# The front of a fused two-block kernel: c alone on ScalarE's queue, an early table load, parameters turned behind x, the third weight tile one piece earlier, and sums of scale and shift by transposes

## The chip, the cores and the metric

The kernel runs on one core of a Trainium2 chip. The metric is the device time of one execution in microseconds, of which the median over several runs is taken. Before the change it is 1377.33 us (three runs, 1375.95 to 1377.88).

## What is computed

Two model blocks on one sequence of 512 tokens with 1024 channels, all float32. Only the first steps matter here:

```python
c_act = jax.nn.silu(c)                                # c: 1 x 1024
mod = (c_act @ w_mod[l] + b_mod[l])[:, None, :]       # w_mod: 1024 x 6144
sh1, sc1, g1, sh2, sc2, g2 = jnp.split(mod, 6, axis=-1)
h = rms_norm(x) * (1.0 + sc1) + sh1                   # x: 512 x 1024
proj = h @ w_in[l]                                    # 1024 x 10272
```

Behind them come a gated branch, a state space scan, three projections, a feed-forward part, and a second block with pooling and a recurrent branch. `sh1` and `sc1` take 8 MB of `w_mod`, and no matmul of `proj` can begin before at least one 128-channel piece of both is known.

## The kernel before

The program is written by hand, engine by engine: each engine has one function (`sp_program`, `pool_program`, `pe_program`, `act_program`, `dve_program`) that lists its instructions in order, and every engine works strictly through its own list. Semaphores tie the lists together. `s_...` names are semaphores; a wait is `wait_ge`.

**Layout.** Channels lie on the 128 partitions, in eight channel groups `m` of 128; tokens lie along the free axis. `XT` is x turned into that form. `h` is kept as two float32r tensors, `Hh` (high part) and `Hl` (the rest), and each weight tile of 1024x128 is split in the same way: `raw[i]` is what the DMA brings, ScalarE rounds it to `whi[i]` (`hi(t)`), VectorE subtracts to `wlo[i]` (`lo(t)`). A product is three matmuls per channel group: whi by Hh, whi by Hl, wlo by Hh. Three such tiles are in flight; the first three of the program (dt, cv 0, cv 1) are tiles 0, 1 and 2.

**The front** is everything up to the last matmul of these three tiles.
- SyncE (SP) issues nearly all loads: x in four pieces (`xnat`), then the pieces of `w_mod` (`wm`) in the order of `MOD_ROWS`, with tiles 0, 1 and 2 put in after pieces 1, 3 and 5 (counted from 0). Pieces 0 to 3 are 512 KB (128 columns each: scale and shift of channel groups 0 and 1), pieces 4 to 9 are 1 MB (256 columns, two channel groups each). Piece 4 is `wm5` (scale) and piece 5 is `wm1` (shift), both for channel groups 2 and 3. ScalarE's own DMA queue brings `c` and, once `c` is there, six small parameter vectors into rows of `pr[1]`.
- TensorE turns c (L808), then x in four calls `x_turned(c)` (L801), and the parameters (L814). `mod_rows(n)` multiplies piece n by silu(c) (L825); it leaves four partial rows in four groups of 32 partitions of a PSUM bank. ScalarE copies that bank to `mrow` (`mod_row(n)`, L1490), and `mod_sums(n)` (L834) multiplies `mrow` by a column `selc` that picks one partition of each group, which both adds the four partials and turns the row into a column. VectorE adds the biases (`h_cols(i)`, L2152 and L2154), scales XT (`h_scaled(m)`, L2166), ScalarE adds the shift and rounds (`h_hi(m)`, L1495), VectorE makes the rest (`h_lo(m)`, L2172).
- `part(t, k...)` (L853 to L855) is tile t's product for the channel groups k, three matmuls each: it waits for `whi`, `wlo`, and for `h_hi(k)` and `h_lo(k)`.
- `keep_busy` (L779) and `keep_busy_half` (L790) are 128x512 bf16 matmuls whose results nobody reads. Their number is written out in TensorE's list.
- The rms of x: ScalarE squares x (L1470), takes the root (L1483), VectorE inverts it (L2145), TensorE spreads it over the partitions (L842).

After the front the general loop `gemm` follows (L742 to L744), with the same three matmuls per channel group.

Of the kernel before, what the change touches and what calls it, by code (L numbers as in the profile page):

```python
# [7 lines left out]
F32R = mybir.dt.float32r  # L8
BF16 = mybir.dt.bfloat16
U8 = mybir.dt.uint8  # L10
ALU = mybir.AluOpType
# [25 lines left out]
def build_program(nc, A, out, blocks):  # L37
# [21 lines left out]
    selc = sb("selc", [P, 2])  # L59
# [55 lines left out]
    filler, = region(106, ("filler", [P, 512], F32R))  # L115
# [329 lines left out]
    def sp_program(sp):  # L445
# [30 lines left out]
        for p, piece in enumerate(MOD_ROWS):  # L476
            load_mod0(*piece)
            if p in (1, 3, 5):
                load((1, 3, 5).index(p))
# [91 lines left out]
    def pool_program(pool):  # L571
# [9 lines left out]
        for i in range(2):  # L581
            pool.tensor_tensor(selc[:, i:i + 1], ident[:, 64 * i:64 * i + 1], ident[:, 64 * i + 32:64 * i + 33],
                               ALU.add).then_inc(s_const, 1)
        pool.wait_ge(s_const, 7)
        pool.tensor_tensor(selc[:, 0:1], selc[:, 0:1], selc[:, 1:2], ALU.add).then_inc(s_const, 1)
        pool.tensor_copy(triub[:, :], triu[:, :]).then_inc(s_const, 1)
        for i in range(4):
            pool.tensor_copy(filler[:, i * 128:(i + 1) * 128], ident[:, :]).then_inc(s_const, 1)
# [127 lines left out]
    def pe_program(pe):  # L716
# [66 lines left out]
        def keep_busy_rounded(n, width, bank=5):  # L783
            for i in range(n):
                pe.matmul(BK[bank][:, 0:width], filler[:, i % 2 * 128:i % 2 * 128 + 128], filler[:, 0:width],
                          start=True, stop=True)

        def keep_busy_half(n, bank=5):
# [4 lines left out]
        def x_turned(c):  # L793
            pe.wait_ge(s_x[c], 16)
            half, at = divmod(c, 2)
            for b in range(4):
                if c == 2 and b == 3:
                    pe.wait_ge(s_pc, 3)
# [7 lines left out]
        keep_busy(4, 0)  # L806
        pe.wait_ge(s_par, 16)
        pe.transpose(BK[5][:, 0:8], pr[1][0:8, :], ident[0:8, 0:8]).then_inc(s_pt, 1)  # L808
        keep_busy(6, 0)
        x_turned(0)  # L810
        x_turned(1)
        pe.wait_ge(s_par, 16 * 7)
        pe.wait_ge(s_cact, 1)
        pe.transpose(BK[5][:, 128:256], pr[1][:, :], ident[:, :]).then_inc(s_pt, 1)  # L814
        x_turned(2)
        x_turned(3)

        def mod_rows(n):
            i, at, width = MOD_ROWS[n]
            if n >= 2:  # L820
                pe.wait_ge(s_mrow, n - 1)
            pe.wait_ge(*((s_wmr[i // 4], 32) if at else (s_wm[i], 16)))
# [6 lines left out]
        def mod_sums(n):  # L829
# [3 lines left out]
            for to, at in [(2 * (n % 2) + n // 2, 0)] if n < 4 else [(2 * n - 4, 0), (2 * n - 3, 128)]:  # L833
                ms = pe.matmul(BK[6][:, to:to + 1], mrow[n % 2][:, at:at + 128], selc[:, 0:1], start=True, stop=True)  # L834
            ms.then_inc(s_ms, 1)

        pe.wait_ge(s_const, 13)
        pe.wait_ge(s_xt0, 4)
        mod_rows(0)
# [19 lines left out]
        mod_rows(1)  # L859
# [2146 lines left out]
```

## Time and profile before

| | |
|---|---|
| median of 3 runs | 1377.33 us |
| the profiled execution's own time | 1375.54 us |
| its span, first to last instruction | 1374.3 us |
| TensorE busy | 1355.8 us, 99% |
| VectorE, ScalarE, GpSimd busy | 65%, 46%, 17% |
| front (last matmul of L855 starts) | at 49.06 us |

The span is 1.24 us shorter than the profiled execution's own time. That execution lies 1.8 us under the median of the three runs. Times in the rows below are microseconds from the start of the span. In the chain of waits a row is a stretch in which that engine, line or transfer is what everything behind it hangs on.

### The profile page before, as it was taken

What the parts mean: (1) busy time and instruction counts of PE and PEld (TensorE: products, weight loads), DVE (VectorE), ACT (ScalarE), POOL (GpSimd) and SP (SyncE); (2) the same over time, 40 slices, a digit from 0 to 9 for tenths busy, and PEclk for the clock granted to TensorE, in tenths of its full rate; (3) what the DMA queues carried; (4) which work ended last, traced back from release to release, by engine and by line L of the source; (5) the groups of instructions that cost most, each with busy time, mean ns of one, the idle gap of its engine ahead of it and who ended that gap; (6) DMA issues with size and microseconds to landing.
All of it is one profiled execution on the core that took longest, in us unless ns stands there. A gap on an engine that the chain in (4) does not pass through costs nothing.

```text
span 1374.3 us, 24508 instructions
## 1 busy us (share of the span) xinstructions
PE 1355.8 (99%) x9502; PEld 1095.3 (80%) x9502; DVE 896.9 (65%) x1274; ACT 628.8 (46%) x1000; POOL 239.9 (17%) x254
## 2 busy tenths in 40 slices
PE   8999999999999999999999999999999999999998
PEld 5788888888887888878888888888888877777776
DVE  4687777887637867784668542334444686867865
ACT  4565555665454523332245432123433465545533
POOL 0000000000037889860022500000000000000220
PEclk9999999999999999999999999999999999999999
DMA  9445344444445676553333333333333232313221
GB/s 346 135 140 140 115 116 130 138 108 128 141 138 157 165 205 195 153 166 95 93 92 93 108 92 108 92 93 94 106 93 92 73 112 60 88 51 92 64 73 77
DMA packets 276009, 163.46 MB, mean 119 GB/s; under 512 B 6573, under 2 KB 264242, under 8 KB 275898
## 3 DMA queue, kind: packets, MB, share of 16 engines
q1 hardware_dynamic: 269530, 158.90, 39.7%
q10 hardware_dynamic: 6368, 3.00, 0.8%
q8 instruction: 79, 1.29, 0.4%
q14 instruction: 32, 0.26, 0.1%
HBM read 159.59 MB, written 2.29 MB: 118 GB/s over the span
## 4 chain that ended last, share of the span: by engine, by line
PE 86%; DVE 6%; ACT 3%; issue 2%; POOL 2%; DMA 1%; ACTq 0%; DVEq 0%; SPq 0%; POOLq 0%
PE PS L742 23%; PE PS L744 22%; PE PS L743 22%; PE PS L942 1%; PE PS L1019 1%; POOL mbuf L607 1%; PE PS L1020 1%; PE PS L1021 1%; PE PS L1354 1%; PE PS L1356 1%; PE PS L1355 1%; PE PS L1257 1%; PE PS L1268 1%; POOL mbuf L602 1%; PE PS L963 1%
## 5 line engine op out<-in xcount | busy, mean ns | idle before, releaser
L742 PE MATMUL PS<-Hh,whi 128*128 128x512 f32 x1096 | 442.8, 404 | 2.6 <-DVE wlo L2113 2.3
L744 PE MATMUL PS<-Hh,wlo 128*128 128x512 f32 x1096 | 427.7, 390 | 0.0
L743 PE MATMUL PS<-Hl,whi 128*128 128x512 f32 x1096 | 427.2, 390 | 0.0
L2113 DVE TENSOR_TENSOR wlo<-raw,whi 128x1024 fp32r<-128x1024 f32 (+2 forms) x211 | 271.8, 1289 | 117.5 <-ACT whi L1457 116.6
L1457 ACT ACTIVATE whi<-raw 128x1024 fp32r<-128x1024 f32 (+2 forms) x215 | 222.6, 1036 | 171.9 <-PE PS L744 121.4
L742 PEld LDWEIGHTS PS<-Hh,whi 128*128 128x128 f32 x1096 | 205.8, 188 | 54.4 <-issue 10.8
L744 PEld LDWEIGHTS PS<-Hh,wlo 128*128 128x128 f32 x1096 | 205.7, 188 | 44.1
L743 PEld LDWEIGHTS PS<-Hl,whi 128*128 128x128 f32 x1096 | 206.1, 188 | 39.6 <-issue 0.7
L602 POOL TENSOR_TENSOR mbuf<-mbuf,cact 128x1024 f32<-128x1024 f32 x32 | 67.4, 2107 | 413.0 <-DMA mbuf<-in_w_mod_dram 407.0
L607 POOL TENSOR_TENSOR mbuf<-mbuf 128x512 f32<-128x512 f32 x68 | 99.7, 1466 | 5.3
L742 PE MATMUL PS<-YBh,whi 128*128 128x512 f32 x256 | 99.6, 389 | 0.0
L743 PE MATMUL PS<-YBl,whi 128*128 128x512 f32 x256 | 99.6, 389 | 0.0
L744 PE MATMUL PS<-YBh,wlo 128*128 128x512 f32 x256 | 99.6, 389 | 0.0
L702 POOL TENSOR_TENSOR pad<-pad 128x512 f32<-128x512 f32 x10 | 11.0, 1097 | 501.7 <-DVE VT L2617 501.2
L2260 DVE SCALAR_TENSOR_TENSOR tmp<-xr,pcA,tmp 128x512 f32<-128x512 f32 x96 | 71.8, 748 | 2.6 <-ACT tmp L1561 0.3
L1591 ACT ACTIVATE dec<-crow,dts 128x128 f32<-128x128 f32 x128 | 44.0, 393 | 31.5 <-PE PS L947 15.0
L742 PEld LDWEIGHTS PS<-YBh,whi 128*128 128x128 f32 x256 | 48.1, 188 | 10.0
L743 PEld LDWEIGHTS PS<-YBl,whi 128*128 128x128 f32 x256 | 48.1, 188 | 9.9
L744 PEld LDWEIGHTS PS<-YBh,wlo 128*128 128x128 f32 x256 | 48.1, 188 | 9.9
L2561 DVE TENSOR_TENSOR tmp<-tmp 128x512 f32<-128x512 f32 x30 | 20.9, 697 | 50.4 <-ACT tmp L1774 50.4
L742 PE MATMUL PS<-R2h,whi 128*128 128x512 f32 x128 | 50.2, 392 | 1.8 <-ACT whi L1457 1.8
L744 PE MATMUL PS<-R2h,wlo 128*128 128x512 f32 x128 | 49.9, 390 | 0.0
(484 smaller groups left out, 1960.2 us busy)
## 6 DMA issues: line engine op xcount, KB each, us to landing
raw<-in_w_in_dram SPq DMA_DIRECT2D x106, 512.0 KB, 3.9
raw<-in_w_ff_dram SPq DMA_DIRECT2D x64, 512.0 KB, 3.7
mbuf<-in_w_mod_dram SPq DMA_DIRECT2D x32, 512.0 KB, 3.9
crow<-cum_rows SPq DMA_DIRECT2D x32, 256.0 KB, 4.6
raw<-in_w_branch_ssm_dram SPq DMA_DIRECT2D x16, 512.0 KB, 3.7
wm<-in_w_mod_dram SPq DMA_DIRECT2D x6, 1024.0 KB, 9.6
erow<-exp_rows SPq DMA_DIRECT2D x24, 256.0 KB, 4.9
raw<-in_w_out_dram SPq DMA_DIRECT2D x9, 512.0 KB, 3.5
```

The lines of the kernel that those rows point to most:

```text
L602: pool.tensor_tensor(w[:, :, :], src[:, :, :], factor.unsqueeze(2).to_broadcast([P, KT, P]), ALU.mult).then_inc(s_pool, 1)
L607: pool.tensor_tensor(w[:, 0:n, :], w[:, 0:n, :], w[:, n:2 * n, :], ALU.add).then_inc(s_pool, 1)
L742: pe.matmul(bank[:, :], whi[s][:, k, :], xh[:, kk, :], start=kk == 0, stop=False)
L743: pe.matmul(bank[:, :], whi[s][:, k, :], xl[:, kk, :], start=False, stop=False)
L744: last = pe.matmul(bank[:, :], wlo[s][:, k, :], xh[:, kk, :], start=False, stop=t == end - 1 and k == (order or range(kt))[-1])
L942: ms = pe.matmul(to(a), xdt[n % 2][:, h * 64:(h + 1) * 64], dec[n % 2][:, h * 128:(h + 1) * 128], start=True, stop=c == 0)
L963: pe.transpose(BK[4][:, j * 128:(j + 1) * 128], F[j][:, sl], ident[:, :])
L1457: act.activation(whi[s][:, 0:kt, :], raw[s][:, 0:kt, :], ACTF.Copy).then_inc(s_whi, 1)
L1591: act.activation(dec[n % 2][:, h * 128:(h + 1) * 128], crow[n % 2][:, h * 128:(h + 1) * 128], ACTF.Relu, bias=CU[:, cc:cc + 1], scale=-1.0 ...
L2113: v.tensor_tensor(wlo[s][:, 0:kt, :], raw[s][:, 0:kt, :], whi[s][:, 0:kt, :].bitcast(F32), ALU.subtract).then_inc(s_wlo, 1)
L2260: e = v.scalar_tensor_tensor(out=a[:, :], in0=b[:, tap:tap + T], scalar=cw(tap, tile), in1=a[:, :], op0=ALU.mult, op1=ALU.add)
L2561: v.tensor_tensor(q, q, q, ALU.mult).then_inc(s_f2, 1)
```

## The change

SyncE's list: the third tile is issued one piece earlier, and the six small parameter loads go from ScalarE's queue to SyncE's, between pieces 0 and 1. ScalarE issues only the load of c; it then runs a dummy Silu, which makes it load that table at once. TensorE no longer runs ten fillers around the turning of c, but four behind it; all four x pieces are turned in one go, the parameters behind them; `mod_rows(0)` and `(1)` now stand together, and the rms is spread behind both. In `mod_sums` the multiplication by `selc` becomes a transpose of 128x128, and the addition of the four partials becomes a VectorE reduction over a stride of 32 (`h_cols`). The counts and places of the later fillers change (6, 3, 9, 2, 4 before, 4, 3, 8, 3 now), `mod_rows(4)`, `(5)` and the parts of tile 2 are interleaved, and GpSimd no longer makes `selc` and an unused filler tile. ScalarE splits tile 2 before it copies row 5.

```diff
--- before.py
+++ after.py
@@ -56,7 +56,6 @@
     triu = sb("triu", [P, P])
     identb = sb("identb", [P, P], BF16)
     triub = sb("triub", [P, P], BF16)
-    selc = sb("selc", [P, 2])
     dcol = sb("dcol", [P, 16])
     pcA = sb("pcA", [P, 128])
     pcB = sb("pcB", [P, 128])
@@ -112,7 +111,6 @@
     wm = region(32, *((f"wm{i}", [P, KT, 256]) for i in range(4)))
     wm += region(73, *((f"wm{i}", [P, KT, 256]) for i in range(4, 8)))
     mrow = region(68, *((f"mrow{i}", [P, 256]) for i in range(2)))
-    filler, = region(106, ("filler", [P, 512], F32R))
 
 
 
@@ -475,8 +473,12 @@
             load_x(c)
         for p, piece in enumerate(MOD_ROWS):
             load_mod0(*piece)
-            if p in (1, 3, 5):
-                load((1, 3, 5).index(p))
+            if p == 0:
+                sp.wait_ge(s_par, 16)
+                for to, ap in fill1[1:]:
+                    sp.dma_start(to, ap).then_inc(s_par, 16)
+            if p in (1, 3, 4):
+                load((1, 3, 4).index(p))
 
         sp.wait_ge(s_wm[3], 16)
         for to, ap in fill2:
@@ -578,14 +580,8 @@
         pool.affine_select(out=triu[:, :], in_=ones[:, :], compare_op=ALU.is_ge, fill=0.0, base=0,
                            pattern=[[1, P]], channel_multiplier=-1).then_inc(s_const, 1)
         pool.tensor_copy(identb[:, :], ident[:, :]).then_inc(s_const, 1)
-        for i in range(2):
-            pool.tensor_tensor(selc[:, i:i + 1], ident[:, 64 * i:64 * i + 1], ident[:, 64 * i + 32:64 * i + 33],
-                               ALU.add).then_inc(s_const, 1)
-        pool.wait_ge(s_const, 7)
-        pool.tensor_tensor(selc[:, 0:1], selc[:, 0:1], selc[:, 1:2], ALU.add).then_inc(s_const, 1)
+        pool.wait_ge(s_const, 4)
         pool.tensor_copy(triub[:, :], triu[:, :]).then_inc(s_const, 1)
-        for i in range(4):
-            pool.tensor_copy(filler[:, i * 128:(i + 1) * 128], ident[:, :]).then_inc(s_const, 1)
         own = 0
         pool.wait_ge(s_cact, 1)
         for q in range(34):
@@ -780,12 +776,8 @@
                           start=True, stop=True)
 
 
-        def keep_busy_rounded(n, width, bank=5):
-            for i in range(n):
-                pe.matmul(BK[bank][:, 0:width], filler[:, i % 2 * 128:i % 2 * 128 + 128], filler[:, 0:width],
-                          start=True, stop=True)
-
-        def keep_busy_half(n, bank=5):
+        def keep_busy_half(n, bank=2):
+            pe.wait_ge(s_const, 6)
             for i in range(n):
                 pe.matmul(h4(BK[bank][:, :]), identb[:, :] if i % 2 else triub[:, :],
                           identb[:, :].unsqueeze(1).to_broadcast([P, 4, P]), start=True, stop=True)
@@ -795,7 +787,7 @@
             half, at = divmod(c, 2)
             for b in range(4):
                 if c == 2 and b == 3:
-                    pe.wait_ge(s_pc, 3)
+                    pe.wait_ge(s_cact, 1)
                 for m in (2 * b, 2 * b + 1):
                     to = m % 2 * 256 + at * 128
                     tr = pe.transpose(BK[X_BANKS[half][b]][:, to:to + 128], xnat[:, c, m * 128:(m + 1) * 128], ident[:, :])
@@ -803,22 +795,18 @@
                     tr.then_inc(s_xtt, 1)
 
         pe.wait_ge(s_const, 5)
-        keep_busy(4, 0)
         pe.wait_ge(s_par, 16)
         pe.transpose(BK[5][:, 0:8], pr[1][0:8, :], ident[0:8, 0:8]).then_inc(s_pt, 1)
-        keep_busy(6, 0)
-        x_turned(0)
-        x_turned(1)
-        pe.wait_ge(s_par, 16 * 7)
-        pe.wait_ge(s_cact, 1)
-        pe.transpose(BK[5][:, 128:256], pr[1][:, :], ident[:, :]).then_inc(s_pt, 1)
-        x_turned(2)
-        x_turned(3)
+        keep_busy(4, 0)
+        for c in range(NC):
+            x_turned(c)
 
         def mod_rows(n):
             i, at, width = MOD_ROWS[n]
             if n >= 2:
                 pe.wait_ge(s_mrow, n - 1)
+            else:
+                pe.wait_ge(s_xt0, n + 1)
             pe.wait_ge(*((s_wmr[i // 4], 32) if at else (s_wm[i], 16)))
             for k in range(KT):
                 q = 32 * (k % 4)
@@ -830,13 +818,13 @@
             pe.wait_ge(s_mrow, n + 1)
             if n >= 2 and n % 2 == 0:
                 pe.wait_ge(s_modc, n)
-            for to, at in [(2 * (n % 2) + n // 2, 0)] if n < 4 else [(2 * n - 4, 0), (2 * n - 3, 128)]:
-                ms = pe.matmul(BK[6][:, to:to + 1], mrow[n % 2][:, at:at + 128], selc[:, 0:1], start=True, stop=True)
+            for to, at in [(n % 2, 0)] if n < 4 else [(n % 2 * 2, 0), (n % 2 * 2 + 1, 128)]:
+                ms = pe.transpose(BK[6][:, to * 128:to * 128 + 128], mrow[n % 2][:, at:at + 128], ident[:, :])
             ms.then_inc(s_ms, 1)
 
-        pe.wait_ge(s_const, 13)
+        mod_rows(0)
+        mod_rows(1)
         pe.wait_ge(s_xt0, 4)
-        mod_rows(0)
         pe.wait_ge(s_xrs, 1)
         for c in range(NC):
             ms = pe.transpose(BK[7][:, c * 128:(c + 1) * 128], small[:, 4 + c:5 + c].to_broadcast([P, P]), ident[:, :])
@@ -856,30 +844,31 @@
             if k == KT - 1:
                 last.then_inc(s_tile, 1)
 
-        mod_rows(1)
         pe.wait_ge(s_xt1, 2)
-        keep_busy(2, 5)
+        pe.wait_ge(s_par, 16 * 7)
+        pe.transpose(BK[5][:, 128:256], pr[1][:, :], ident[:, :]).then_inc(s_pt, 1)
         mod_sums(0)
         mod_sums(1)
-        keep_busy_half(6)
+        pe.wait_ge(s_xt0, 6)
+        keep_busy_half(4)
         mod_rows(2)
         keep_busy_half(3)
         mod_rows(3)
-        pe.wait_ge(s_xt0, 6)
         part(0, 0)
         mod_sums(2)
         mod_sums(3)
-        keep_busy_half(9)
+        keep_busy_half(8)
         part(1, 0)
         part(0, 1)
+        mod_rows(4)
         part(1, 1)
-        mod_rows(4)
         mod_rows(5)
-        keep_busy_half(2)
+        part(2, 0)
         mod_sums(4)
         mod_sums(5)
-        keep_busy_half(4)
-        part(2, 0, 1)
+        part(2, 1)
+        pe.wait_ge(s_pc, 3)
+        keep_busy_half(3, 5)
         mod_rows(6)
         part(0, 2, 3)
         mod_rows(7)
@@ -1470,9 +1459,8 @@
             act.activation(xs[:, c, :], xnat[:, c, :], ACTF.Square, accum_out=small[:, 4 + c:5 + c]).then_inc(s_rx, 1)
 
         act.dma_start(*fill1[0]).then_inc(s_par, 16)
-        act.wait_ge(s_par, 16)
-        for to, ap in fill1[1:]:
-            act.dma_start(to, ap).then_inc(s_par, 16)
+        act.wait_ge(s_pc, 1)
+        act.activation(small[:, 63:64], EPS, ACTF.Silu)
         act.wait_ge(s_pt, 1)
         act.activation(cact[:, :], BK[5][:, 0:8], ACTF.Silu).then_inc(s_cact, 1)
         act.wait_ge(s_pc, 2)
@@ -1506,8 +1494,8 @@
         hi(1)
         h_hi(1)
         mod_row(4)
+        hi(2)
         mod_row(5)
-        hi(2)
         for j in range(1, 4):
             h_hi(2 * j)
             h_hi(2 * j + 1)
@@ -2134,25 +2122,25 @@
             v.wait_ge(s_xtt, 4 * half + b + 1)
             v.tensor_copy(x_half(b, half), x_bank(b, half)).then_inc(s_xt0, 1)
 
-        for b in range(2):
+        for b in range(4):
             x_copy(b, 0)
+        v.wait_ge(s_rx, 5)
+        v.reciprocal(small[:, 4:8], small[:, 4:8]).then_inc(s_xrs, 1)
+        x_copy(0, 1)
+        x_copy(2, 1)
         v.wait_ge(s_pt, 2)
         cols_of(BK[5][:, 128:256], pcB, 128, 1.0)
-        for b in range(2, 4):
-            x_copy(b, 0)
-        x_copy(0, 1)
-        v.wait_ge(s_rx, 5)
-        v.reciprocal(small[:, 4:8], small[:, 4:8]).then_inc(s_xrs, 1)
-        x_copy(2, 1)
 
         def h_cols(i):
             m, n = (i, 1) if i < 2 else (2 * i - 2, 2)
-            at = m if i < 2 else 2 * m
+            total = small[:, 32:32 + 2 * n]
             v.wait_ge(s_ms, 2 * i + 2)
-            v.scalar_tensor_tensor(out=opc[:, m:m + n], in0=BK[6][:, at:at + n], scalar=1.0,
+            own(v.tensor_reduce(total, BK[6][:, 0:256 * n].rearrange("p (b g r) -> p b g r", g=4, r=32)[:, :, :, 0],
+                                mybir.AxisListType.X, ALU.add))
+            v.wait_ge(s_dve, nown)
+            v.scalar_tensor_tensor(out=opc[:, m:m + n], in0=total[:, 0:n], scalar=1.0,
                                    in1=colr("b_mod", 8 + m, n), op0=ALU.add, op1=ALU.add).then_inc(s_modc, 1)
-            v.tensor_tensor(modc[:, m:m + n], BK[6][:, at + 2:at + 2 + n], colr("b_mod", m, n),
-                            ALU.add).then_inc(s_modc, 1)
+            v.tensor_tensor(modc[:, m:m + n], total[:, n:2 * n], colr("b_mod", m, n), ALU.add).then_inc(s_modc, 1)
 
         def h_scaled(m):
             v.wait_ge(s_modc, 2 * of_cols(m) + 1)
```

**SyncE's list, from the second piece of `w_mod` to the seventh.** `wm` are the pieces of `w_mod`, `raw` the weight tiles, `pr1` the parameter rows. Before:

```order
L472 DMA wm0<-in_w_mod_dram 128x8x128
L457 DMA raw1<-in_w_in_dram 128x8x128
L472 DMA wm5<-in_w_mod_dram 128x8x256
L472 DMA wm1<-in_w_mod_dram 128x8x256
L457 DMA raw2<-in_w_in_dram 128x8x128
L472 DMA wm6<-in_w_mod_dram 128x8x256
```

Now, and ahead of it the six loads that came from ScalarE's queue:

```order
L479 DMA pr1<-in_b_mod_dram 48x128
L479 DMA pr1<-in_conv_b_dram 32x128
L479 DMA pr1<-in_gm_norm_w_dram 8x128
L479 DMA pr1<-in_ssm_norm_w_dram 16x128
L479 DMA pr1<-in_final_norm_w_dram 8x128
L479 DMA pr1<-in_norm_gain_2_dram 8x128
...
L470 DMA wm5<-in_w_mod_dram 128x8x256
L455 DMA raw2<-in_w_in_dram 128x8x128
L470 DMA wm1<-in_w_mod_dram 128x8x256
L470 DMA wm6<-in_w_mod_dram 128x8x256
```

`raw2` and `wm1` have changed places, and six small loads stand between the first two pieces of `w_mod`.

**TensorE's list around pieces 4 and 5 (`wm5` and `wm1`).** `mrow0` and `mrow1` are the copied rows of the two pieces, `whi2` and `wlo2` belong to tile 2. Before:

```order
L825 MATMUL PS<-wm5,cact 32x256 x8
L825 MATMUL PS<-wm1,cact 32x256 x8
L790 MATMUL PS<-identb,triub 128x512
L790 MATMUL PS<-identb 128x512
L834 MATMUL PS<-selc,mrow0 128x1 x2
L834 MATMUL PS<-selc,mrow1 128x1 x2
L790 MATMUL PS<-identb,triub 128x512
L790 MATMUL PS<-identb 128x512
L790 MATMUL PS<-identb,triub 128x512
L790 MATMUL PS<-identb 128x512
L853 MATMUL PS<-Hh,whi2 128x512
L854 MATMUL PS<-Hl,whi2 128x512
```

Now:

```order
L813 MATMUL PS<-wm5,cact 32x256 x8
L841 MATMUL PS<-Hh,whi1 128x512
L842 MATMUL PS<-Hl,whi1 128x512
L843 MATMUL PS<-Hh,wlo1 128x512
L813 MATMUL PS<-wm1,cact 32x256 x8
L841 MATMUL PS<-Hh,whi2 128x512
L842 MATMUL PS<-Hl,whi2 128x512
L843 MATMUL PS<-Hh,wlo2 128x512
L822 MATMUL PS<-ident,mrow0 128x128 x2
L822 MATMUL PS<-ident,mrow1 128x128 x2
```

A part of tile 1 now stands between the two pieces and a part of tile 2 behind them, the six fillers around the sums are gone, and the sums are transposes. Behind these rows come the other part of tile 2 and three fillers, and then, as before, piece 6 and the parts of tile 0.

**VectorE's list at channel groups 2 and 3.** Before:

```order
L2113 TENSOR_TENSOR wlo2<-raw2,whi2 128x1024
L2152 SCALAR_TENSOR_TENSOR opc<-PS,pcB 128x2
L2154 TENSOR_TENSOR modc<-PS,pcB 128x2
L2166 SCALAR_TENSOR_TENSOR tmp2<-XT,opc,PS 128x512
L2166 SCALAR_TENSOR_TENSOR tmp0<-XT,opc,PS 128x512
```

Now:

```order
L2101 TENSOR_TENSOR wlo2<-raw2,whi2 128x1024
L2138 TENSOR_REDUCE small<-PS 128x4
L2141 SCALAR_TENSOR_TENSOR opc<-small,pcB 128x2
L2143 TENSOR_TENSOR modc<-small,pcB 128x2
L2154 SCALAR_TENSOR_TENSOR tmp2<-XT,opc,PS 128x512
L2154 SCALAR_TENSOR_TENSOR tmp0<-XT,opc,PS 128x512
```

One reduction has been added ahead of the two bias instructions, and the first of these waits for it.

## Rows read from the trace of the kernel before

**Rows 1.** The page: span, engines, and the chain that ended last by engine.
```profile
span 1374.3 us, 24508 instructions
...
PE 1355.8 (99%) x9502; PEld 1095.3 (80%) x9502; DVE 896.9 (65%) x1274; ACT 628.8 (46%) x1000; POOL 239.9 (17%) x254
...
PE 86%; DVE 6%; ACT 3%; issue 2%; POOL 2%; DMA 1%; ACTq 0%; DVEq 0%; SPq 0%; POOLq 0%
```

**Rows 2.** Busy time in one stretch: engines, granted TensorE clock, DMA share, GB/s.
```profile
20.00:25.00 5.00, 4.75 (x43) 2.61 (x43) 1.95 (x3) 0.93 (x2) 0.00 (x0) 1.00 1.11 375
```

**Rows 3.** Chain of waits in order of time, 23 to 50: start, length, what.
```profile
23.73 1.86 PE PS L825 x32
...
30.98 0.43 PE PS L853
...
34.47 0.79 PE PS L834 x8
35.25 0.34 PE PS L853
...
38.41 0.43 PE PS L853
...
48.23 0.92 issue
```

**Rows 4.** Timeline of SyncE's issues (start, length of the issue), pieces wm1, raw2, wm3.
```profile
15.14 1.45 SPq L472 DMA_DIRECT2D wm<-in_w_mod_dram  x1
...
16.64 1.60 SPq L457 DMA_DIRECT2D raw<-in_w_in_dram  x1
...
25.97 2.55 SPq L472 DMA_DIRECT2D wm<-in_w_mod_dram  x1
```

**Rows 5.** DMA view of the same three issues: the last number is issue to landing.
```profile
wm<-in_w_mod_dram SPq DMA_DIRECT2D x1, 1024.0 KB, 9.2
...
raw<-in_w_in_dram SPq DMA_DIRECT2D x1, 512.0 KB, 9.2
...
wm<-in_w_mod_dram SPq DMA_DIRECT2D x1, 1024.0 KB, 10.8
```

**Rows 6.** Timeline of ScalarE and VectorE from 25.6 to 30 (start, length, instruction, idle before).
```profile
25.66 0.38 ACT L1490 ACTIVATE mrow<-PS 128x256 f32<-128x256 f32 x1 [0.48 <-PE PS L825]
25.94 1.05 ACT L1457 ACTIVATE whi<-raw 128x1024 fp32r<-128x1024 f32 x1
...
27.02 1.23 DVE L2113 TENSOR_TENSOR wlo<-raw,whi 128x1024 fp32r<-128x1024 f32 x1 [5.07 <-ACT whi L1457]
28.16 0.15 DVE L2152 SCALAR_TENSOR_TENSOR opc<-PS,pcB 128x2 f32<-128x2 f32 x1
28.35 1.41 DVE L2166 SCALAR_TENSOR_TENSOR tmp<-XT,opc,PS 128x512 f32<-128x512 f32 x2
29.89 1.42 DVE L2172 SCALAR_TENSOR_TENSOR Hl<-tmp,modc,Hh 128x512 fp32r<-128x512 f32 x2
```

**Rows 7.** Timeline of the first 13 us: ScalarE, VectorE, TensorE.
```profile
4.52 0.33 ACTq L1475 DMA_DIRECT2D pr<-in_norm_gain_dram  x1
4.89 1.28 ACT L1477 ACT_TABLE_LOAD   x1 [4.89 <-DMA pr<-in_norm_gain_dram]
...
12.40 0.18 DVE L2145 RECIPROCAL small<-small 128x4 f32<-128x4 f32 x1 [0.51 <-ACT small L1483]
...
4.36 2.74 PE L779 MATMUL PS<-identb 128*128 128x512 bf16 x6
```

**Rows 8.** Chain of waits: turning rms and parameters, and fillers at 19 us.
```profile
12.63 0.65 PE PS L842 x4
...
19.18 1.96 PE PS L790 x9
...
44.86 0.11 PE PS L900
44.98 0.19 PE PS L901
```

## What the change will do to the time

> **What bounds the kernel now.** I read the page first: the span is 1374.3 us, TensorE is busy for 99% of it and carries 86% of the chain that ended last [rows 1]. The change touches only the front, the first 49 us, so the question is how much earlier TensorE can leave the front; behind it the same work follows, with TensorE full. The windows come second: between 20 and 25 us the DMA engines are full at 375 GB/s and TensorE is busy 4.75 of 5 us, part of it with fillers [rows 2]. So two things can bound the front: the stream of x, `w_mod` and tiles, and TensorE's own backlog. The chain of waits tells where one takes over from the other [rows 3]. From `mod_rows(4)` and `(5)` at 23.73 on, TensorE waits for data or runs fillers until it starts tile 2. The `part(0, 2)` that begins at 30.98 is the first product of channel groups 2 and 3. From there to the wait at 48.23 the chain shows TensorE alone, one matmul behind the other: this is backlog, 17.3 us of it. Last the SyncE issues with their landings [rows 4, 5] and the timeline of ScalarE and VectorE between 25 and 30 us [rows 6] show what held 30.98: `wm1` landed at 15.14 + 9.2 = 24.34, `raw2` at 16.64 + 9.2 = 25.84; ScalarE rounded `raw2` only then (25.94, 1.05 us), VectorE subtracted at 27.02 for 1.23 us, and the bias instruction stood behind that at 28.16, though its sums had long been ready.
>
> So the front has two terms: the moment at which `part(0, 2)` can start (30.98 now), and the length of the backlog behind it.
>
> **The change part by part.**
>
> *The first 20 us.* ScalarE loses six issues of some 0.33 us, its table load (1.28 us, at 4.89) goes beside the load of c, and so silu(c) and the squares of x come 2 to 3 us earlier; the root then waits for the last piece of x instead [rows 7]. TensorE loses six of its ten early fillers and several later ones. I cost all of this at nothing. What hides it is the stream: pieces 2 to 5 land when they land, and `wm1` is the one that 30.98 hangs on. A gain here turns into a longer wait for `wm1`. If that cover were gone, the 1.28 us of the table load would be the upper end of a gain.
>
> *Six small loads on SyncE's queue.* They stand ahead of `wm0`, together 120 rows of 512 bytes, 61 KB. As bytes they are 0.16 us at 375 GB/s [rows 2], and before they shared the same engines from the other queue, so the lower end is 0. Their issues cost SyncE 6 x 0.33 = 2.0 us [rows 7]; if the stream stood still meanwhile, everything behind would be 2.0 us late, the upper end. I take 0.1: landings run some 9 us behind their issues [rows 4, 5], so the engines have work queued while SyncE issues these.
>
> The Trainium skill (DMA: Bandwidth & Descriptors, "Issuing engines are not separate DMA queues") says that issues from several engines run on the same DMA engines and save only the issuer's time. By it the move changes no landing and this term is 0; its sum would be 0.1 us lower than mine. No row before shows a small load in front of a large one in one queue, so its own advice that transfers under 64 KB are mostly overhead (same page, "Rules for kernel authors") speaks for the late side; that is priced in the second rival.
>
> *`raw2` before `wm1`.* The bytes ahead of the later of the two are the same. So `raw2` now lands with `wm5` plus 0.5 MB, and `wm1` takes the 25.84 of `raw2`, with the 0.1 from above 25.94. The splitting of tile 2 (1.05 and 1.23 us) falls into the time before. What is late next is the way from `wm1` to `part(0, 2)`:
> - `mod_rows(5)`: 1.86 / 2 = 0.93 [rows 3], to 26.9; 0.07 later `mrow` for 0.38 [rows 6], to 27.35;
> - two transposes: four took 0.65 in the spreading of the rms [rows 8], two less at 0.11 each [rows 8] make 0.43, to 27.8;
> - the reduction, which no row shows on this shape: bounds 0.15 (the bias instruction) and 0.38 (a copy of 256 columns), taken as 0.18 like the reciprocal on four columns [rows 6, 7], plus 0.05 for its hand-over, to 28.05;
> - bias to scaling 0.19 (28.16 to 28.35), scaling to the first `Hl` 1.54, and that `Hl` 0.71 (half of 1.42) [rows 6]: 28.05 + 0.19 + 1.54 + 0.71 = 30.5.
>
> TensorE itself is there at about the same time: sums done at 27.8, `part(2, 1)` 3 x 0.23, three fillers 3 x 0.22 (nine took 1.96 [rows 8]), `mod_rows(6)` 0.93 and the two changes of kind at 0.2 each (0.43 against 0.23 [rows 3]): 30.5. With 0.2 for hand-overs that I can't see, `part(0, 2)` starts at 30.7 instead of 30.98: -0.3 us. Bounds: -0.6 with no such losses, +0.4 with the reduction at its upper end and both hand-overs doubled.
>
> *The sums in the backlog.* Two double sums stand behind 30.98. Each takes 0.79, and the matmul behind it 0.34 [rows 3]: 1.13. Four transposes at 0.11 to 0.19 [rows 8] are 0.44 to 0.76, the matmul behind them 0.43 [rows 3]: 0.87 to 1.19. I take the near one, 0.11, since transposes in a row are what is issued here: 2 x -0.26 = -0.5 us; bounds -0.6 and +0.1. The reduction on VectorE lengthens the way to channel group 4 by 0.2 to 0.4. It is covered: bias 0.03 after the sums, at 35.29, plus 0.19 + 1.54 + 0.71 is 37.7, and the first `part` of group 4 stands at 38.41 [rows 3], 0.7 later.
>
> *Behind the front.* The wait at 48.23 [rows 3] is one for ScalarE's copies behind the last parts; it moves with them. Nothing else changes.
>
> Sum: 0 - 0.3 - 0.5 = -0.8 us. On the profiled execution's own time of 1375.54 that is 1374.7; that execution lies 1.8 under the median of the runs, so I put the same -0.8 on the median: 1377.33 - 0.8 = 1376.5.
>
> **The rivals.**
>
> *The clock of TensorE stays low (slower).* The six fillers at 4.36 took 2.74 us, about 0.43 each; the nine at 19.18 took 1.96, 0.22 each [rows 7, 8]. So the engine ran at the lower of its two levels, 1.2 GHz, in its first microseconds and at 2.4 GHz later, where the granted clock reads 1.00 [rows 2], after a stretch of dense fillers. The change leaves four of ten and then turns x in four bursts between landings. If the rise comes later, all up to `wm1` (25.9) is covered: TensorE waits or runs fillers in much of it, and a slower engine only fills that time. It decides only from about 23 us on. Still low until 30.7, it would double `mod_rows(5)`, `part(2, 0)`, the sums, `part(2, 1)`, the fillers and `mod_rows(6)`: 0.93 + 0.7 + 0.44 + 0.7 + 0.66 + 0.93 = 4.4, less the 0.3 and 0.5: +3.6, 1380.9. Against it speaks that parts and fillers are dense from 13 us on. The Trainium skill (TensorE: Matmul & The Clock Gate, Part 1) has the throttled clock as the default and activity as what releases it, which is the reason why thinning out the fillers is a risk; the rows agree in that the first fillers are the slow ones. Chance 0.07.
>
> *The small loads hold the stream.* With the 2.0 us in full, `wm1` lands at 27.8, `part(0, 2)` starts at 32.6, +1.6, and with the -0.5: +1.1, 1378.4. For it: small loads in front of large ones. Against: SyncE's issue runs far ahead of the landings (9.2 us). Chance 0.14.
>
> *Nothing gained.* Hand-overs and the transposes eat both terms; +0.4 and +0.1 are their ends: about 1377.5. Chance 0.16.
>
> *More than the two terms.* The stream was 0.3 to 0.5 us late because of the other queue, and the hand-overs are free: `part(0, 2)` at 30.0, sums -0.6: -1.6, 1375.7. The end beyond which nothing goes is the last piece: `wm3` lands at 25.97 + 10.8 = 36.8 [rows 4, 5]; 0.93 + 0.07 + 0.38 + 0.65 + 0.23 + 0.19 + 1.54 + 0.71 later, at 41.5, the last products could start, six parts at 0.69 end at 45.6, against some 49.3 now. This -3.7 would take a backlog that is gone, and the backlog starts with `wm1`. Chance 0.13 for -1.6, 0.02 for more.
>
> **How the numbers follow.** 0.48 for the forecast, 0.07, 0.14, 0.16 and 0.15 for the rest. A measurement of this kernel can tell about 0.2% from no change, 2.75 us: below 1374.6 counts as faster, above 1380.1 as slower. Nearly every case lies between. For faster I take 0.10 (the large gain, and the spread of the medians, whose three runs lie 1.9 us apart), for slower 0.09 (the clock, and the same spread), for no change 0.81. The range from 1374.4 to 1379.3 holds the forecast, the three middle cases and a microsecond of spread at either end; it leaves out the clock case.
>
> **What would show it.** The profile after should have: the table load ahead of 2 us and the root of the squares near 10.5; `raw2` landing near 23 and `wm1` near 25.9; TensorE idle or waiting for 1 us or more just before `mod_rows(5)`; the first `part` of channel group 2 of tile 0 near 30.7; about 0.5 us in the chain at each double sum of transposes instead of 0.79; and the wait behind the front near 47.4 instead of 48.23. I am wrong if `wm1` lands past 26.5, if matmuls of 512 columns still stand 0.43 apart past 22 us, if a double sum with its next matmul takes over 1.1 us, or if the front ends early and the end of the span doesn't follow.

## The result and the profile after

The changed kernel is slower: 1380.34 us median of 7 runs (1378.03 to 1382.09) against 1375.95 of the kernel before on the same chips; the ratio is 1.0034, 95% interval 1.0023 to 1.0046. The forecast was 1376.5 us, in a range of 1374.4 to 1379.3. The execution that was profiled took 1382.09 us, the longest of the seven; the profiled one of the kernel before took 1375.54. So the two profiles lie further apart than the medians, 6.55 against 4.39 us.

The page of the changed kernel, the lines that answer to [rows 1]:

```profile
span 1380.7 us, 24453 instructions
...
PE 1355.1 (98%) x9472; PEld 1093.9 (79%) x9472; DVE 894.0 (65%) x1279; ACT 628.9 (46%) x1001; POOL 239.5 (17%) x247
...
PE 85%; DVE 5%; issue 3%; ACT 2%; POOL 2%; DMA 1%; SPq 1%; ACTq 0%; DVEq 0%; POOLq 0%
```

The span is 6.4 us longer, and TensorE has not become busier. The chain of waits of the changed kernel from 18 to 55 us (start, length, what) shows where most of it arises, 4.5 us by the end of the front:

```profile
18.06 11.27 DMA wm<-in_w_mod_dram
29.33 0.14 issue
29.46 1.82 PE PS L813 x16
31.29 0.73 PE PS L841
32.01 0.43 PE PS L842
32.44 0.43 PE PS L843
32.87 0.60 PE PS L822 x4
...
36.34 0.47 PE PS L841
...
52.76 0.93 issue
```

`part(0, 2)` starts at 36.34; it was 30.98 [rows 3] and forecast at 30.7. From there to the wait behind the front it is 16.4 us, where it was 17.25: the backlog shrank, as forecast, and its start moved by 5.4 us. Two rows name the reasons. First, the chain hangs on `wm1`, which lands at 18.06 + 11.27 = 29.33 and not at 25.9. Second, `mod_rows(5)` takes 1.82 us instead of 0.93, the matmuls of 512 columns behind it 0.43 instead of 0.23.

The second is the clock. The windows of the changed kernel (columns as in [rows 2]):

```profile
12.00:16.00 4.00, 3.11 (x25) 2.42 (x26) 0.46 (x2) 1.33 (x2) 0.00 (x0) 0.57 1.21 294
25.00:29.40 4.40, 1.01 (x7) 0.48 (x3) 1.23 (x1) 1.44 (x2) 0.00 (x0) 1.00 1.09 348
29.50:33.00 3.50, 3.50 (x21) 2.05 (x22) 0.00 (x0) 0.38 (x1) 0.00 (x0) 0.52 1.09 348
```

TensorE was busy for 1.0 of 4.4 us while it waited for `wm1`, and behind that the granted clock was 0.52: 1.2 GHz for most of 3.5 us. It had been low once before, from 12 to 16 us (0.57), behind waits of 0.96 and 1.86 us for the first pieces; there the waits for the stream that follow cover it.

The first is the stream. These are its issues on SyncE (start, length of the issue: `wm5`, `raw2`, `wm1`), and the DMA view of the same three (last number: issue to landing), which answer to [rows 4, 5]:

```profile
14.23 2.00 SPq L470 DMA_DIRECT2D wm<-in_w_mod_dram  x1
16.28 1.74 SPq L455 DMA_DIRECT2D raw<-in_w_in_dram  x1
18.06 1.97 SPq L470 DMA_DIRECT2D wm<-in_w_mod_dram  x1
```
```profile
wm<-in_w_mod_dram SPq DMA_DIRECT2D x1, 1024.0 KB, 8.8
...
raw<-in_w_in_dram SPq DMA_DIRECT2D x1, 512.0 KB, 10.1
...
wm<-in_w_mod_dram SPq DMA_DIRECT2D x1, 1024.0 KB, 11.3
```

`raw2` lands at 16.28 + 10.1 = 26.4, over 3 us later than the forecast's 23, though the list is the one that was forecast. The DMA engines were not idle meanwhile. The DMA view from 12 to 16 us, when nearly all packets are rows of 512 bytes, of the kernel before and then of the changed one:

```profile
DMA packets 2736, 1.38 MB, mean 344 GB/s; under 512 B 47, under 2 KB 2736, under 8 KB 2736
...
q1 hardware_dynamic: 2736, 1.38, 114.1%
```
```profile
DMA packets 2333, 1.18 MB, mean 294 GB/s; under 512 B 36, under 2 KB 2333, under 8 KB 2333
...
q1 hardware_dynamic: 2333, 1.18, 120.9%
```

The share times 16 engines times 4 us, divided by the packets, is the time of one: 26.7 ns before, 33.2 ns after. Each row costs a quarter more. An estimate from these numbers says whether that is enough: up to `wm1` the stream has seven loads in rows of 512 bytes (four pieces, three tiles, 7168 rows), which is 7168 x 6.5 ns / 16 = 2.9 us, and two of 1 MB in rows of 1 KB, at 348 instead of 386 GB/s 0.6 us more. Together that is 3.5 us, and `wm1` came 3.4 us late.

The order of the engines' lists doesn't explain why a row should cost more. What does is a line that had no part in the forecast: `selc = sb("selc", [P, 2])` is gone. Tensors are laid out one behind the other. `selc` took 8 bytes per partition, and since the next tensor, `dcol`, begins on a multiple of 32, everything from `dcol` on lay 32 bytes further than it does now. By the addresses in the built programs, before the change `raw`, `wm` and `xnat` begin on multiples of 256 bytes (`raw[0]` at 36864 = 144 x 256), and after it 224 past one (36832). A row of 512 bytes then lies across three blocks of 256 instead of two.

The Trainium skill (DMA: Bandwidth & Descriptors, "How a descriptor splits into AXI transactions") says that a descriptor which doesn't start on a multiple of 256 bytes gets a first transaction from the multiple below its start, and that the unused bytes of it still cost. The trace agrees in that such a row takes 33.2 instead of 26.7 ns. It doesn't follow in size: with 64 and 128 unused bytes instead of 224 a row still takes 32.1 and 32.4 ns (experiment 3).

The rest of the 6.4 us arises behind the front. The cumulative sums start at 69.00 where they started at 64.24, 4.8 us later, and in the second block the difference has grown to 6.0 us:

```profile
1171.62 0.43 PE L1305 MATMUL PS<-CS,Pb 128*128 128x64 f32 x2 [0.97 <-issue]
```

In the kernel before the same matmuls stand at 1165.59 without a wait. What this wait is for is not shown.

### The profile page after: what moved, and what is told of

It is laid out like the page before. It is cut to its first block, busy times and chain, and to the rows that moved or that the text cites. A ratio compares the mean times of both kernels' runs of the same rounds, so it can differ in the third digit from the quotient of the medians.

```text
span 1380.7 us, 24453 instructions
## 1 busy us (share of the span) xinstructions
PE 1355.1 (98%) x9472; PEld 1093.9 (79%) x9472; DVE 894.0 (65%) x1279; ACT 628.9 (46%) x1001; POOL 239.5 (17%) x247
## 4 chain that ended last, share of the span: by engine, by line
PE 85%; DVE 5%; issue 3%; ACT 2%; POOL 2%; DMA 1%; SPq 1%; ACTq 0%; DVEq 0%; POOLq 0%
PE PS L738 22%; PE PS L740 21%; PE PS L739 21%; PE PS L931 1%; PE PS L1008 1%; PE PS L1009 1%; PE PS L1010 1%; PE PS L1343 1%; POOL mbuf L603 1%; PE PS L1345 1%; PE PS L1344 1%; PE PS L1246 1%; PE PS L1257 1%; DMA wm<-in_w_mod_dram 1%; POOL mbuf L598 1%
## 5 line engine op out<-in xcount | busy, mean ns | idle before, releaser
L603 POOL TENSOR_TENSOR mbuf<-mbuf 128x512 f32<-128x512 f32 x68 | 95.0, 1398 | 5.3
L738 PEld LDWEIGHTS PS<-YBh,whi 128*128 128x128 f32 x256 | 48.0, 188 | 10.1
```

The source lines that it names most:

```text
L603: pool.tensor_tensor(w[:, 0:n, :], w[:, 0:n, :], w[:, n:2 * n, :], ALU.add).then_inc(s_pool, 1)
L738: pe.matmul(bank[:, :], whi[s][:, k, :], xh[:, kk, :], start=kk == 0, stop=False)
```

## The experiments

Ratios are to the kernel before, with 95% intervals. "Front" is the start of the first general matmul behind the front in the profiled execution, 49.77 before and 54.30 in the changed kernel.

**1. The changed kernel with the 32 bytes back.**

```diff
     triub = sb("triub", [P, P], BF16)
+    gap = sb("gap", [P, 2])
```

> The changed kernel with 32 bytes per partition of unused memory where selc was (selc had moved all that lies behind it; it is gone in the change, and raw, wm and xnat now start 224 bytes past a multiple of 256 instead of on one). Placement theory: 512-byte rows of a DMA are again some 27 ns instead of 33, the two pieces before mod_rows(5) land near 24.4 and 25.9 us instead of 26.3 and 29.3, no stretch of TensorE at 1.2 GHz behind 20 us, first part of channel groups 2 and 3 near 30.7, time 1374.5 to 1376 (ratio to before 0.999 to 1.000). Rival (the six small loads on SyncE's queue slow the stream): wm1 still lands at 29 us, ratio 1.003. Rival (bursts of turning x and fewer fillers): clock still drops near 30 us, ratio 1.001 to 1.003.

Measured: 1.0002 (0.9993 to 1.0011), 1375.92 us. Nobody reads or writes these bytes, and the loss is gone within the interval. From 12 to 16 us a row is back at 26.7 ns (DMA view, 12 to 16 us):

```profile
DMA packets 2755, 1.39 MB, mean 347 GB/s; under 512 B 48, under 2 KB 2755, under 8 KB 2755
...
q1 hardware_dynamic: 2755, 1.39, 114.9%
```

The chain of this kernel, 15 to 49 us:

```profile
15.98 9.70 DMA wm<-in_w_mod_dram
25.68 0.14 issue
25.81 1.94 PE PS L814 x16
27.75 0.73 PE PS L842
...
32.54 0.47 PE PS L842
...
36.08 0.44 PE PS L823 x4
36.52 0.23 PE PS L842
...
49.04 0.92 issue
```

`wm1` lands at 25.68, as forecast. But `mod_rows(5)` again takes 1.94 us: in the 4 us from 25 to 29 the granted clock is 0.57 (TensorE alone: busy time, granted clock, DMA share, GB/s):

```profile
25.00:29.00 4.00, 3.19 (x19) 0.57 1.08 386
```

Ahead of it TensorE had waited 2.04 us for that landing. So the time agrees with the placement theory, and its expectation on the clock failed in this execution. Only one more of the eleven runs has a mean granted clock as low as this one's 0.998; the others have 0.999 or 1.000.

**2. The kernel before with its memory shifted.**

```diff
     cact = sb("cact", [P, 8])
+    gap = sb("gap", [P, 56])
```

> The kernel before with 224 bytes per partition of unused memory ahead of raw, so that raw, wm and xnat start at the same 224 bytes past a multiple of 256 as in the changed kernel; nothing else differs. Placement theory: 512-byte rows take 33 ns, wm3 lands some 4 us later than 36.7, ratio to before 1.002 to 1.004. Rivals (small loads, order of pieces, fillers): no difference, ratio 1.000.

Measured: 1.0016 (1.0007 to 1.0025), 1378.07 us; front 52.82, and a row costs 33.7 ns (121.3% of 16 engines, 2303 packets):

```profile
q1 hardware_dynamic: 2303, 1.16, 121.3%
```

Placement alone makes the old kernel slower. The ratio is below the 1.002 to 1.004 that was expected; the interval reaches into it.

**3. Which boundary it is.** The changed kernel with 96 and with 160 bytes of unused memory in the same place (`[P, 24]`, `[P, 40]` in experiment 1's line): tensors begin 64 and 128 past a multiple of 256.

> The changed kernel with 96 bytes of unused memory: raw, wm and xnat start 64 bytes past a multiple of 256. If what matters is the boundary of 256 bytes (the Trainium skill, DMA: Bandwidth & Descriptors, How a descriptor splits into AXI transactions), this is as slow as the changed kernel, ratio 1.003. If a boundary of 64 bytes is enough, it is as fast as with 32 bytes, 0.999 to 1.000.

> The changed kernel with 160 bytes of unused memory: raw, wm and xnat start 128 bytes past a multiple of 256. By the 256-byte rule 1.003, by a 64-byte or 128-byte rule 0.999 to 1.000.

Measured: 1.0034 (1.0022 to 1.0047) and 1.0027 (1.0017 to 1.0038). Tensors that begin on a multiple of 64 or 128 bytes, but not of 256, are as slow. (The profiled execution with 160 bytes took 1377.19 us, the second shortest of its eight.) The DMA view from 12 to 16 us, of the one and of the other, gives 32.1 and 32.4 ns:

```profile
q1 hardware_dynamic: 2325, 1.17, 116.6%
```
```profile
q1 hardware_dynamic: 2354, 1.19, 119.3%
```

**4. Fillers in the idle stretch**, in the kernel of experiment 1 (eight of them) and in the changed kernel itself (sixteen):

```diff
         part(1, 1)
+        keep_busy_half(8)
         mod_rows(5)
```

> The changed kernel with the 32 bytes of unused memory, and eight fillers of 128x512 on TensorE in the idle 2 us ahead of mod_rows(5). In the run with the 32 bytes alone TensorE ran at 1.2 GHz from 25.5 to 28.9 us and part(0, 2) started at 32.54. Clock theory: without that idle stretch the clock stays at 2.4 GHz, part(0, 2) starts at 30.7 to 30.9, the wait behind the front comes at 47.2 to 47.4, ratio to before 0.9985 to 0.9995. Rival (the low clock is chance, or comes from something earlier): as without the fillers, 1.000, low clock in the twenties.

> The changed kernel itself, with its memory as it is, and sixteen fillers of 128x512 on TensorE in the idle 3.4 us ahead of mod_rows(5). Clock theory: the stream is as late as in the changed kernel (wm1 at 29.3), but no stretch of 1.2 GHz near 30 us, the front 1.5 to 2 us earlier than in the changed kernel, ratio to before 1.0018 to 1.0025. If placement alone makes all of the loss: 1.0034 as before.

Measured: 1.0009 (1.0000 to 1.0018) and 1.0038 (1.0026 to 1.0051). In both profiles the clock stays at 2.4 GHz through the front, which ends at 49.18 and 52.49, 1.4 and 1.8 us earlier than without fillers. The times do not follow: neither ratio is below that of the kernel without fillers, and both expectations (0.9985 to 0.9995, 1.0018 to 1.0025) failed.

The runs themselves say more of the clock than the profiles. All seven runs of the changed kernel have a mean granted clock of 0.996 to 0.998, and the five with sixteen fillers have 0.998 to 1.000, like the kernel before. So the low clock is no accident of one profile; but with it gone the ratio is still 1.0038, so no share of the loss is shown to be its.

Two profiles of experiment 3 show that the length of the wait alone doesn't decide it. With 160 bytes TensorE waited 2.4 us for `wm1` at that place, longer than the 2.0 us of experiment 1, and the granted clock stayed up; with 96 it waited 2.8 us and the clock fell. The wait in the first of these two (TensorE's timeline, then the windows):

```profile
28.44 0.85 PE L814 MATMUL PS<-wm,cact 128*32 128x256 f32 x12 [2.41 <-DMA wm<-in_w_mod_dram]
```
```profile
24.00:28.50 4.50, 2.09 (x24) 1.00 1.10 348
```

The first kernel of this experiment also shows what can take a shorter front's gain. Its chain from 24 to 65 us:

```profile
24.26 1.74 PE PS L783 x8
26.00 1.00 PE PS L814 x16
...
46.56 6.56 DMA bsb<-in_gm_bs_dram
...
53.81 0.76 DVE tmp L2250
...
63.77 0.24 DVE dts L2224
...
64.29 0.46 PE PS L909 x2
```

The chain no longer runs through the end of the front but through the load of `bsb`, 512 KB, behind which VectorE's dt and convolution work waits until 53.1, and through that work to the cumulative sums at 64.29. In the kernel before these stand at 64.24 in TensorE's own list:

```profile
64.24 0.46 PE PS L918 x2
```

The 0.6 us that the front had gained are gone there. But the two executions drift apart again behind it: at 610 us the one with fillers is 0.9 us ahead, then its clock falls. TensorE's list in the kernel before, in the one with fillers, and there the window behind (TensorE alone):

```profile
610.97 0.47 PE L742 MATMUL PS<-R2h,whi 128*128 128x512 f32 x1 [1.77 <-ACT whi L1457]
```
```profile
610.05 0.47 PE L739 MATMUL PS<-R2h,whi 128*128 128x512 f32 x1 [1.83 <-ACT whi L1448]
```
```profile
611.00:614.50 3.50, 3.50 (x10) 0.51 0.73 215
```

With 3.5 us of busy work at half the clock, by estimate 1.7 us, the lead is lost. Both executions waited some 1.8 us there, and only one had the low clock behind it (so had the one with 96 bytes in experiment 3, 0.53 from 616 to 619.5 us). Differences of a microsecond between the ends of single profiles therefore say nothing about the front.

**5. The load of `bsb` later**, in the kernel before and in the first kernel of experiment 4. The wait for the small loads of `bc`, which stood in one count with `bsb`, no longer includes it (names cut short with `...`):

```diff
-        sp.dma_start(bsb[:, :, :], A["gm_bs"]...).then_inc(s_par2, 16)
...
+            if t == tile0[("z", 0)] + 8:
+                sp.wait_ge(s_par2, N_BC)
+                sp.dma_start(bsb[:, :, :], A["gm_bs"]...).then_inc(s_par2, 16)
-    N_BC, N_WS, ... = N_PAR2 + 64, N_PAR2 + 80, ...
+    N_BC, N_WS, ... = N_PAR2 + 48, N_PAR2 + 80, ...
```

> The kernel before, with the 512 KB load of bsb issued some tiles later (it is first read at 425 us) and the wait for the small bc loads no longer held by it. In the kernel before bsb lands at 53.1 and VectorE's dt and convolution work starts only then; but TensorE's own list reaches the cumulative sums at 64.24 at about the same time. Theory: VectorE starts that work near 50.5 us, TensorE is bound by its own list, so the time changes little: ratio 0.9992 to 1.0002, first cumulative sum (two matmuls with triu and ones) at 63.6 to 64.2. Rival (bsb holds nothing): VectorE's work starts at 53 as before.

> The changed kernel with the 32 bytes of unused memory, the eight fillers ahead of mod_rows(5), and the load of bsb issued some tiles later. With the first two alone the front was 0.6 us shorter than before (first general matmul at 49.18 instead of 49.77), and at 64.3 us nothing was left of it, because VectorE had waited for bsb until 53.1. Theory: now the 0.6 us stays, cumulative sums at 63.4 to 63.7 instead of 64.24, ratio 0.9990 to 1.0000, 0.0005 to 0.0010 below the kernel without the later bsb. Rival (the gain is lost elsewhere): 64.2 again, ratio 1.0005.

Measured: 0.9998 (0.9989 to 1.0007) and 0.9999 (0.9990 to 1.0008). VectorE's work starts at 52.2 instead of 53.2 in both, a smaller step than expected. In the second it now waits for the last small load of `bc`, in the first the profile names TensorE's turning of dt. The cumulative sums did not come earlier: their second pair of matmuls starts at 64.69 and 64.59, where it was 64.53. In the second `wm1` happened to land 0.9 us later than in experiment 4 and the front ended at 50.0, so its test failed: whether the 0.6 us stays once `bsb` is out of the way is not shown. It has the lowest ratio of all versions of the change that I ran, and is no faster than the kernel before.

**6. The small loads back on ScalarE's queue**, with the 32 bytes:

```diff
-            if p == 0:
-                sp.wait_ge(s_par, 16)
-                for to, ap in fill1[1:]:
-                    sp.dma_start(to, ap).then_inc(s_par, 16)
...
         act.activation(cact[:, :], BK[5][:, 0:8], ACTF.Silu).then_inc(s_cact, 1)
+        act.wait_ge(s_par, 16)
+        for to, ap in fill1[1:]:
+            act.dma_start(to, ap).then_inc(s_par, 16)
```

> The changed kernel with the 32 bytes of unused memory, and the six small parameter loads back on ScalarE's queue, behind silu(c). Theory that they cost nothing on SyncE's queue: wm1 lands at 25.6 within 0.3 us, ratio 1.000. Rival (small loads ahead of large ones hold the stream): wm1 lands 0.5 to 2 us earlier.

Measured: 1.0004 (0.9995 to 1.0013). `wm1` lands at 26.1 (17.74 + 8.39 in its chain), 0.45 us later than in experiment 1 and not earlier. So no delay by the small loads in front of the large ones shows.

```profile
17.74 8.39 DMA wm<-in_w_mod_dram
```

**7. The sums by transposes alone, in the kernel before.** Only `mod_sums` and `h_cols` are taken over from the change:

```diff
-                ms = pe.matmul(BK[6][:, to:to + 1], mrow[n % 2][:, at:at + 128], selc[:, 0:1], start=True, stop=True)
+                ms = pe.transpose(BK[6][:, to * 128:to * 128 + 128], mrow[n % 2][:, at:at + 128], ident[:, :])
...
+            own(v.tensor_reduce(total, BK[6][:, 0:256 * n].rearrange("p (b g r) -> p b g r", g=4, r=32)[:, :, :, 0],
+                                mybir.AxisListType.X, ALU.add))
```

> The kernel before with the sums of scale and shift by transposes and the reduction on VectorE, and nothing else of the change. Forecast for this part was -0.5 us in the backlog; the traces of the changed kernel show 0.44 + 0.24 us for a double sum and the next matmul instead of 0.79 + 0.34, so now 2 x -0.45 = -0.9 us from 30.98 to 48.23, less up to 0.3 us at part(0, 2). Ratio 0.9993 to 0.9998, wait behind the front at 47.3 to 47.6. Rival (the reduction and its hand-over eat it): 1.000, 48.2.

Measured: 1.0001 (0.9992 to 1.0010). Front 49.67 instead of 49.77; the wait behind it at 48.13. This run's stream was late (`raw2` at 16.88 + 9.7 = 26.6 instead of 25.8), which took the backlog's gain back. A double sum takes 0.44 us; a gain of the kernel, expected at 0.9993 to 0.9998, is not shown.

**8. The third tile behind `wm1` again**, with the memory of the changed kernel and with the 32 bytes:

```diff
-            if p in (1, 3, 4):
+            if p in (1, 3, 5):
...
-        hi(2)
         mod_row(5)
+        hi(2)
...
         mod_rows(5)
-        part(2, 0)
+        keep_busy_half(2)
         mod_sums(4)
         mod_sums(5)
-        part(2, 1)
-        pe.wait_ge(s_pc, 3)
-        keep_busy_half(3, 5)
+        keep_busy_half(4)
+        part(2, 0, 1)
```

> The changed kernel with its memory as it is, but with tile 2 behind wm1 again, as in the kernel before (SyncE's issues, ScalarE's row 5 ahead of the splitting of tile 2, TensorE's parts of tile 2 behind the sums with six fillers around these). The kernel before with shifted memory lost 0.16%, the changed one 0.34%. Theory that the earlier tile makes the rest, since it puts wm1 last in a stream that is 3 us late: wm1 lands near 27, ratio 1.001 to 1.002. Rival (small loads, fillers, bursts of x): 1.0035 as in the changed kernel.

> The same with the 32 bytes of unused memory, so with the memory of the kernel before. With the earlier tile it was 1.0002. Theory: with the stream on time both orders end at the same landing (25.8), ratio 0.9995 to 1.0002, first general matmul at 49.2 to 49.8. Rival (the earlier tile gains by itself): 1.0005 or more, 50.2 or later.

Measured: 1.0022 (1.0013 to 1.0031) and 1.0005 (0.9996 to 1.0015); fronts 51.53 and 48.69. With shifted memory the ratio is 1.0022 where the changed kernel has 1.0034, though the intervals overlap. With aligned memory both orders are within the noise of 1. The profile with the 32 bytes has a front 1.1 us shorter than that of the kernel before, but it is the shortest of its eleven runs (1373.82 us), and the ratio of 1.0005 doesn't show it. In this execution `bsb` landed earlier too, though its load had not been moved, and 0.9 of the 1.1 us were still there at the cumulative sums (VectorE, then TensorE):

```profile
52.33 0.29 DVE L2191 TENSOR_TENSOR dts<-PS,bc 128x128 f32<-128x128 f32 x1 [2.91 <-DMA bsb<-in_gm_bs_dram]
...
63.37 0.46 PE L907 MATMUL PS<-dts,triu 128*128 128x128 f32 x2 [0.21 <-DVE dts L2222]
```

## Why the prediction was wrong

**The step that failed** is "The bytes ahead of the later of the two are the same [...] `wm1` takes the 25.84 of `raw2`". It took the time of a landing from the bytes ahead of it and so assumed that a row costs what it had cost. The diff's first hunk changed that: 32 bytes less ahead of all destinations, 33.2 instead of 26.7 ns for 512 bytes. `wm1` came 3.4 us late (29.33 for 25.94). Experiments 1 to 3 show this as the cause: put back, the bytes take the ratio from 1.0034 to 1.0002; applied to the old kernel, the shift makes 1.0016; multiples of 64 and 128 don't help. None of the rivals had it. The second one (the small loads hold the stream) had the right symptom with the wrong cause, which experiments 1 and 6 exclude.

**Why the changed kernel loses twice what the old one loses to the same shift** (1.0034 against 1.0016). With the third tile behind `wm1` again it is 1.0022, which speaks for the order: in the change the landing that everything hangs on is also the last of the two, with the long way over row, sums, scaling and rounding behind it, while before it was a tile, with only its splitting behind it. The intervals overlap (1.0013 to 1.0031, 1.0023 to 1.0046), and experiment 8 changed fillers and ScalarE's order along with the tile, so I call this likely, not shown. In the profiles the front is 4.5 us longer in the one and 3.1 in the other, the span 6.4 and 2.5; what the changed kernel loses behind its front is unexplained.

**The first 20 us** were costed at nothing, and that held: experiment 1 has all of it and no loss. Silu, root and squares came early (table load at 1.42, root at 9.49, where it was 12.07), and TensorE waited for the stream instead.

**The small loads on SyncE's queue**: 0.1 us taken; no cost is shown, though their six issues took 3.3 us of SyncE's time and not 2.0.

**The way from `wm1` to `part(0, 2)`** was forecast at 4.8 us (25.9 to 30.7). At 2.4 GHz (first kernel of experiment 4) it measured 26.00 to 31.2, 5.2 us: `part(2, 0)` between the piece and its sums takes 0.9 and the sums start at 27.90, where I had 27.35. So this term is +0.2 instead of -0.3. The reduction itself was right (0.17 us, and 0.2 with its hand-over).

**The sums in the backlog**: forecast -0.5, bounds -0.6 and +0.1; measured 0.44 + 0.23 instead of 0.79 + 0.34 per double sum, 2 x -0.46 = -0.9. The matmul behind transposes costs 0.23, not the 0.43 that I took.

**Behind the front** I wrote that nothing else changes. That failed too: a load that the front doesn't hold, `bsb`, can take its gain. In experiment 4 it landed at 53.1 and the -0.6 us of the front were 0 at 64.3; in experiment 8 it landed at 52.3 and 0.9 of 1.1 us remained. With memory in place the change is at 1.0002 (experiment 1), so neither the forecast -0.8 us nor its absence can be told from the times.

**The clock rival** (0.07) happened in the profiled execution, through an idle stretch and not through the missing early fillers, and at half its forecast price: 1.8 us of front. The mean clocks of all seven runs point to it, but taking it away (experiment 4) gained nothing in the times.

## What to carry to other kernels

Before a loss is sought in the order of instructions, compare the time of one DMA packet of the same size in both traces; where it differs, look at the addresses. Removing or adding a small tensor ahead of the destinations of loads is a change of its own: keep those on multiples of 256 bytes, or give the removed tensor's bytes back. And a stage that ends earlier may gain only up to the next load that doesn't move with it, so the row behind the stage has to be read as well. Where the gain sought is a microsecond, one profile of each kernel can't show it at the end of the span.

## What the runs showed of the hardware

- Rows of 512 bytes into SBUF cost 26.7 ns each on multiples of 256 bytes and 32 to 34 ns at 64, 128 and 224 bytes past one, with 16 engines busy (344 to 347 against 291 to 297 GB/s). Rows of 1 KB still moved at 348 instead of 386 GB/s, while for the loads of x, in rows of 4 KB, no loss is seen: x's last square, which waits for the last of them, started at 8.31 with shifted memory and at 8.27 with the 32 bytes back.
- Three profiled executions had a stretch of 1.2 GHz behind TensorE's wait for `wm1`: of 2.0 us (experiment 1), 2.8 us (96 bytes, experiment 3) and 3.5 us (the changed kernel). One with 2.4 us (160 bytes) had none there, nor had experiment 2 with 1.7 us and experiment 6 with 1.1 us. Behind the wait of 1.8 us at 610 us the clock fell in the first kernel of experiment 4 and not in the kernel before. The runs don't show what decides.
- Six loads of 4 to 24 KB ahead of large ones in one queue delayed these by nothing that shows: `wm1` landed at 25.7 with them (experiment 1) and at 26.1 without (experiment 6).
